# A state-space scan whose barred places are added by TensorE, with its rows loaded a stage earlier, and an expert combination with six slots

## The reference, cut to what matters

```python
def ssd_scan(x, dt, A, Bm, Cm):
    a_cs = jnp.cumsum(dt * A, axis=2)
    seg = a_cs[:, :, :, None, :] - a_cs[:, :, None, :, :]
    mask = jnp.tril(jnp.ones((CHUNK, CHUNK), dtype=bool))[:, :, None]
    Lmat = jnp.exp(jnp.where(mask, seg, -jnp.inf))
    xdt = x * dt[..., None]
    scores = jnp.einsum('bclhn,bcshn->bclsh', Cm, Bm) * Lmat
    y_diag = jnp.einsum('bclsh,bcshp->bclhp', scores, xdt)
    states = jnp.einsum('bclhn,bclh,bclhp->bchpn', Bm, decay_to_end, xdt)
    ...
    y_off = jnp.einsum('bclhn,bchpn,bclh->bclhp', Cm, prev, jnp.exp(a_cs))
# the end: two expert rows per token, weighted, gated, added to h, normalised
out = jnp.zeros((T, D)).at[row_tok].add(row_w[:, None] * yb)
h = h + gate2 * out
y = rmsnorm(h, final_g)
```

## Time and profile before

| | us | of the span |
|---|---|---|
| PE busy | 2977.3 | 82% |
| DVE (VectorE) busy | 2391.4 | 66% |
| ACT (ScalarE) busy | 1554.2 | 43% |
| POOL (GpSimd) busy | 558.5 | 15% |
| scan's stage, first instruction to the backward carry | 1601.2 to 1925.5 | 9% |
| combination, first load to the end | 3488.2 to 3628.8 | 4% |

### The profile page before, as it was taken

One profiled execution on the slowest core, in us unless ns is written; L12 is line 12 of the kernel. 1 busy time (PEld: TensorE's weight loads), 2 busy tenths in 40 slices (PEclk: granted clock), 3 DMA queues, 4 the chain that ended last, 5 costly groups with the idle time before them and its releaser, 6 DMA issues. The chain is left out here.

```text
span 3628.8 us, 41802 instructions
## 1 busy us (share of the span) xinstructions
PE 2977.3 (82%) x12653; PEld 1939.6 (53%) x12653; DVE 2391.4 (66%) x2967; ACT 1554.2 (43%) x1752; POOL 558.5 (15%) x413
## 2 busy tenths in 40 slices
PE   6999999489999999967783799819999999999920
PEld 3666666334444444434442455407777777777720
DVE  2555555347777777748996344347887888887855
ACT  2323332013333333343221122107788777777743
POOL 0000000000000000006660000042222222222224
PEclk8999999669999999988985899859999999999965
DMA  6112121521011110120005233345577776568347
GB/s 241 47 38 66 46 54 42 171 41 33 21 35 35 32 34 20 29 87 1 0 0 190 96 120 117 113 174 188 211 255 265 289 264 234 203 249 313 114 169 275
DMA packets 238793, 445.74 MB, mean 123 GB/s; under 512 B 22658, under 2 KB 96478, under 8 KB 237966
## 3 DMA queue, kind: packets, MB, share of 16 engines
q1 hardware_dynamic: 222141, 397.16, 32.6%
q0 software_dynamic: 16592, 47.84, 3.7%
HBM read 366.93 MB, written 86.40 MB: 125 GB/s over the span
## 5 line engine op out<-in xcount | busy, mean ns | idle before, releaser
L2090 DVE TENSOR_TENSOR weights_rest<-w,weights_rounded 128x2048 fp32r<-128x2048 f32 x314 | 716.3, 2289 | 191.8 <-ACT weights_rounded L2025 191.7
L2025 ACT ACTIVATE weights_rounded<-w 128x2048 fp32r x314 | 598.4, 1913 | 148.6 <-PE ps_up L1949 93.8
L823 ACT ACTIVATE probs<-ps_scores 128x1024 f32<-128x1024 f32 x260 | 266.1, 1023 | 503.8 <-PE ps_scores L754 442.0
L846 DVE TENSOR_REDUCE part_max<-ps_max 128x1 f32<-128x512 f32 (+1 forms) x528 | 338.0, 678 | 193.8 <-PE ps_max L731 193.7
L1949 PE MATMUL ps_up<-weights_rounded,block_T_rounded 128*128 128x512 f32 x832 | 339.6, 408 | 28.5 <-DVE weights_rest L2090 24.0
L430 PE MATMUL ps_proj<-w_in,n1T 128*128 128x512 f32 (+2 forms) x1152 | 348.0, 460 | 6.5 <-PEq L108 6.5
L1949 PE MATMUL ps_up<-weights_rounded,block_T_rest 128*128 128x512 f32 x832 | 327.4, 394 | 0.0
L1949 PE MATMUL ps_up<-weights_rest,block_T_rounded 128*128 128x512 f32 x832 | 326.1, 392 | 0.0
L764 PE MATMUL ps_attn<-probs,v 128*64 128x512 f32 x1040 | 283.7, 625 | 0.0
L430 PEld LDWEIGHTS ps_proj<-w_in,n1T 128*128 128x128 f32 x1152 | 197.8, 193 | 144.9 <-issue 130.0
L1498 PE MATMUL ps_out<-x_and_B,mix_T 128*128 128x512 f32 x576 | 255.7, 603 | 11.2 <-DVE mix_T L1539 11.2
(11 more groups left out here) (335 smaller groups left out, 4695.4 us busy)
## 6 DMA issues: line engine op xcount, KB each, us to landing
w<-in_w SPq DMA_DIRECT2D x96, 2048.0 KB, 10.7
expert_rows<-scratch_y SPq DMA_DIRECT2D x36, 512.0 KB, 5.0
w_ada_rest<-in_w_ada SPq DMA_DIRECT2D x5, 2048.0 KB, 16.0
scratch_qT<-qT_stage SPq DMA_DIRECT2D x18, 512.0 KB, 3.5
q_for_max<-scratch_qT SPq DMA_DIRECT2D x36, 256.0 KB, 5.7
q_rounded_twice<-scratch_qT SPq DMA_DIRECT2D x36, 256.0 KB, 4.3
mix_rows<-scratch_mix SPq DMA_DIRECT2D x18, 512.0 KB, 4.3
scratch_h<-h_rows SPq DMA_DIRECT2D x18, 512.0 KB, 2.6
```

What stands on the lines that cost most here:

```text
L823: act.activation(pf[:, slot(p, n), :], ps_s[:, n % 2, :], ACT.Exp).then_inc(exp_done, 1)
L846: nc.vector.tensor_reduce(mx[:, p, n // H, n % H:n % H + 1], ps_m[:, n % 2, 0:PART], AX.X, ALU.max).then_inc(m_taken, 1)
L2025: act.activation(split_piece(wh, s), raw_piece(s, buf[0]), ACT.Copy).then_inc(hi_done, 1)
L2090: nc.vector.tensor_tensor(split_piece(wl, s), raw_piece(s, buf), split_piece(wh, s).bitcast(F32), ALU.subtract).then_inc(lo_done, 1)
```

## The change

Three things. (1) The rows, masks and small constants of the scan are loaded in sample attention, behind its first three loads, into memory set aside before it; each channel group has a semaphore of its own, and SiLU stands before the exponentials of the sums. (2) `segment` and `mask` are gone. PE adds to the spread sums a matrix with 0 at allowed and -1e9 at barred places (rounded identity times `barred`, broadcast over four heads), and ScalarE takes the exponential per head with the row's negative sum as bias. `weights` multiplies by the unmasked C times B, which `rows` now takes from PSUM too. (3) The combination has six slots and is written out tile by tile; the tile's weights are read where they lie.

```diff
@@ attention_phase, SP
             load_for_max(1, 1)
+            if g:
+                load_scan(sp)
+        def load_scan(sp):
+            for name in ("dt_bias", "a_log", "d_skip"): ...
+            for c in range(XC):
+                for a, b, col in ((0, S_PROMPT, CONV_BASE[0]), (S_PROMPT, T, CONV_BASE[1])):
+                    sp.dma_start(dst, rows[:, c, col:col + b - a]).then_inc(S["ssm_in"][c], 16)
@@ ssm_phase, ScalarE
             own.link(act.activation(work[:, 3], work[:, 2], ACT.Ln))
+            for c in range(XC):
+                act.wait_ge(loaded[c], 32)
+                act.activation(v, v, ACT.Silu).then_inc(silu_done, 1)
             act.wait_ge(sums_ready, 3)
...
             def exps(c, p, d):
-                act.wait_ge(seg_ready, c * 2 + d + 1)
-                act.activation(e[:, p, d], e[:, p, d], ACT.Exp).then_inc(e_ready, 1)
+                act.wait_ge(sm_ready, c + 1)
+                act.wait_ge(bc_ready, c * 2 + d + 1)
+                wait(act, yd_ready, c - 1)
+                for h in range(H):
+                    last = act.activation(e[:, p, d, h, :], b_a[:, h * P:(h + 1) * P], ACT.Exp, bias=sm[:, p, NACS, d * H + h:d * H + h + 1])
+                last.then_inc(e_ready, 1)
@@ ssm_phase, PE: spread
-                wait(pe, seg_ready, c * 2 + d)
+                wait(pe, e_ready, c * 2 + d)
                 for n in range(2):
+                    nc.tensor.matmul(b_a[...], masks[:, 2, :], sacs[...], start=True, stop=False)
+                    last = nc.tensor.matmul(b_a[...], identr[:, :], bars, start=False, stop=True)
@@ ssm_phase, VectorE
+            nc.vector.tensor_copy(identr[:, :], S["ident"][:, :])
+            nc.vector.tensor_scalar(barred[:, :, :], masks[:, 0:2, :], -1.0, 1.0e9, ALU.add, ALU.mult)
+            nc.vector.tensor_scalar(stats[:, :, NACS, :], stats[:, :, ACS, :], -1.0, None, ALU.mult)
...
                 if more:
                     stage(c + 1, 1 - p)
-                    mask(c + 1, 1 - p)
-                    segment(c + 1, 1 - p, 0)
                 carry_on(c, p)
                 if more:
-                    segment(c + 1, 1 - p, 1)
                     weights(c + 1, 1 - p, 0)
                     weights(c + 1, 1 - p, 1)
                 add_up(c, p)
@@ combine_phase
+    RING = 6
             load(0)
             ...
+            for t in range(NT):
+                if t + RING - 1 < NT:
+                    load(t + RING - 1)
+                sp.wait_ge(o_ready, t + 1)
+                sp.dma_start(dst, o[:, t % RING, :]).then_inc(stored[t % RING], 16)
```

More of the change, by code:

```diff
@@ L914, in ssm_phase @@
     HG = SSM_H // SSM_G
-    ACS, EA, DT, DTDE, CD = range(5)
+    ACS, EA, DT, DTDE, CD, NACS = range(6)
     with ctx:
@@ L953, in ssm_phase @@
         block = ctx.enter_context(nc.Block())
[L954 to L967, removed]
         @block.gpsimd
@@ L1226, in _ @@
             stage(0, 0)
-            mask(0, 0)
-            for d in range(2):
-                segment(0, 0, d)
             for d in range(2):
@@ L2142, in _ @@
                 rest_weights(i, 13, after)
-def tiles_by_three(eng):
-    for t in range(3):
-        yield t, t, 0
-    with eng.Fori(1, NT // 3 - 1) as i:
-        for u in range(3):
-            yield i * 3 + u, u, i
-    for t in range(NT - 3, NT):
-        yield t, t % 3, t // 3
 def combine_phase(nc, I, S, R, O):
     ctx = ExitStack()
+    RING = 6
     with ctx:
@@ L2224, in _, with weigh @@
             own = Tally(act, act_own)
-            def weigh(t, p, turn):
-                act.wait_ge(y_in[p], turn * 32 + 32)
-                act.wait_ge(ws_ready, t + 1)
-                act.activation(y[:, p, 0, :], y[:, p, 0, :], ACT.Identity, scale=ws[:, p, 0:1]).then_inc(a_ready, 1)
-            weigh(0, 0, 0)
-            for t, p, turn in tiles_by_three(act):
-                own.at(t)
-                if at := ahead(t, p, turn, 1):
-                    weigh(*at)
+            def weigh(t):
+                act.wait_ge(y_in[t % RING], 32 * turn(t))
+                act.activation(y[:, t % RING, 0, :], y[:, t % RING, 0, :], ACT.Identity, scale=S["weights"][:, 0, t:t + 1]).then_inc(a_ready, 1)
@@ L2236, in _ @@
+            weigh(0)
+            for t in range(NT):
+                if t + 1 < NT:
+                    weigh(t + 1)
                 act.wait_ge(res_ready, t + 1)
-                own.link(act.activation(junk[:, :], o[:, p, :], ACT.Square, accum_out=st[:, p, 0:1]))
-                act.activation(st[:, p, 1:2], st[:, p, 0:1], ACT.Sqrt, scale=1.0 / D, bias=S["eps"][:, :]).then_inc(st_ready, 1)
+                own.link(act.activation(junk[:, :], o[:, t % RING, :], ACT.Square, accum_out=st[:, t % 3, 0:1]))
+                act.activation(st[:, t % 3, 1:2], st[:, t % 3, 0:1], ACT.Sqrt, scale=1.0 / D, bias=S["eps"][:, :]).then_inc(st_ready, 1)
@@ L2264, in _ @@
+            add_rows(0)
+            for t in range(NT):
+                if t + 1 < NT:
+                    add_rows(t + 1)
+                dve.wait_ge(gated, t + 1)
+                dve.wait_ge(h_in[t % RING], 16 * turn(t))
+                wait(dve, stored[t % RING], 16 * (t // RING))
+                nc.vector.tensor_tensor(o[:, t % RING, :], yg[:, t % 3, :], h[:, t % RING, :], ALU.add).then_inc(res_ready, 1)
+                if t == 0:
+                    dve.wait_ge(consts_in, 48)
                 dve.wait_ge(st_ready, t + 1)
-                nc.vector.reciprocal(st[:, p, 2:3], st[:, p, 1:2]).then_inc(inv_ready, 1)
+                nc.vector.reciprocal(st[:, t % 3, 2:3], st[:, t % 3, 1:2]).then_inc(inv_ready, 1)
```

164 lines of the change are left out of this document (72 added, 92 removed).

## The result

The changed kernel took 3575.79 us (median of 4 runs, 3574.65 to 3579.04) against 3635.12 (4 runs, 3630.17 to 3638.28) for the kernel before: a ratio of 0.9839, 95% interval 0.9822 to 0.9856. The forecast was 3579. The profiled execution after has a span of 3574.0 us, 54.8 less than before.

| us | before | after | forecast |
|---|---|---|---|
| preparation, barrier to GpSimd's first block of C | 35.2 | 20.7 | -14.4, came -14.5 |
| loop, from there to the end of the last y | 288.9 | 275.7 | -19, came -13.2 |
| combination | 140.6 | 119.3 | -18.5, came -21.3 |
| all other stages, whose work is unchanged | 3164.1 | 3158.3 | 0, came -5.8 |

A forecast was written before the change was run, and what follows sets the result against it. It took GpSimd's pass with its waits to set the scan's chunk and VectorE's round the new combination: 3630.65 - 14.4 - 19 - 18.5 = 3578.8, predicted 3579 us, with 8 in 10 runs from 3558 to 3598.

The forecast's parts named there:

- preparation: Scan's preparation: early loads and SiLU ahead of the exponentials start GpSimd's first chunk sooner, -14.4 us (-13 to -15).
- loop: Scan's loop: GpSimd's pass with its waits sets a chunk, 14.4 us against 15.5, so -19 us (0 to -32).
- combination: Combination: loads five tiles ahead leave VectorE's round, 5.70 us a tile against 6.79, so -18.5 us (0 to -20).
- rival D: Sample attention: its second tile's q waits behind the moved loads, giving back up to 20 us; 3593 us, chance 0.06.
- the 45 us of the first tile: Sample attention: tile 1 begins over 45 us after tile 0, covering the moved loads' 20 us, so cost 0.
- rival B: Loop: the port does not hold up the weights; PE's 13.5 us sets the chunk, -34 us, 3564 us; chance 0.14.
- -1.1, over 17 steps: Loop: each chunk falls from 15.5 to 14.4 us, -1.1, over 17 steps -19 us.
- 9.26 + 1.4: Loop, GpSimd's pass a chunk: 9.26 us of its own uncontended work plus 1.4 pushed in by VectorE's operations.
- rival E: Loop: PE becomes the bound at a granted clock below 0.78 and the kernel gets slower, up to 3793 us; chance 0.05.
- 13.5: Loop: PE's busy us a chunk at full granted clock with four added products, up from 12.54 (13.0 to 14.3).
- 349 GB/s: Combination: DMA rate worked out as 304/0.87, making a tile's transfers 6.0 us, 0.3 longer than VectorE's round.
- rival C: Combination: bound by the DMA engines, share 0.87 near full, so no gain there; 3597 us, chance 0.14.

The follow-up runs named there:

- experiment 6: Changed kernel with GpSimd's fifth scaled copy of x (the skip copy) made by ScalarE in eight small copies: 3567.57 us.
- experiment 9: Changed kernel with GpSimd's diagonals made in two operations, one for each direction, each with its own semaphore: 3545.69 us.
- experiment 12: Changed kernel with the diagonals in halves, the skip copy on ScalarE and the combination's gate on VectorE, together: 3517.15 us.
- experiment 2: Changed kernel with three slots in the combination in place of six, still written out tile by tile: 3598.12 us.
- experiment 4: Changed kernel with the second-row addition moved into VectorE's wait for the root, and the gate multiplication moved from GpSimd to VectorE: 3566.73 us.
- experiment 3: Changed kernel with VectorE's second-row addition of the next tile moved into its wait for ScalarE's root: 3585.25 us.

## Why the prediction was right

The three stages together came 49.0 us shorter, where the sum had 51.9; the combination's 2.8 made up half of the loop's shortfall of 5.8, and the unchanged stages added 5.8 that no step claimed. So the closeness of 3575.79 to 3579 is in part luck, and the terms are the better test.

**Preparation: right, -14.5 for -14.4.** The chain of single durations held (SiLU done at 1613.4, 17.2 us after the barrier, as worked out). Sample attention did not pay: 838.5 us with the 16 loads in its queue, 838.8 before, so rival D is out. That the 45 us of the first tile cover the loads fits this and was not tested.

**Loop: the mechanism right, the size not: -13.2 for -19.** GpSimd's pass with its waits was the thing to follow (experiments 6, 9 and 12), weights wait for GpSimd (2661 ns, so rival B is out), and ScalarE's pass is 2.17 for 2.2. The term that was mis-sized is "-1.1, over 17 steps". By the rows above, GpSimd's pass is 151.77/15 = 10.1 us busy, where the forecast had 9.26 + 1.4; 3.8 of waiting for the statistics, for 3.7; and 9.5/15 = 0.6 of waiting for PE, which the forecast put at nothing: 14.5 in all, for 14.4. The first 15 steps after the first y took 218.6 us in place of 232.6, so 14.0 less where the forecast had 16.5; two of them took 16.0 and 15.9 after PE's wait and lower clock, some 3 us together. The last two were never 15.5 long: 12.5 and 7.9 before, 11.4 and 9.2 after. The very last ran at a granted clock of 0.57; in two kernels with the same scan (experiments 2 and 4) it took 6.2 at 1.00, and their loops are 17 us shorter than before. So part of the shortfall is this profile's luck. The forecast priced the clock only as a disaster (rival E), not as a small toll inside the steps. E did not come: the granted clock was 0.94 over 216 us, with PE busy for 187.35 of them.

PE's "13.5" a chunk was too high, though the sum did not use it: the kernel with all three of experiment 12 keeps the bars and takes 11.7 us a step. So what rival B would have given is priced too low, and at full granted clock the margin of GpSimd's pass over PE was larger than the forecast thought.

That VectorE's two clamps, 4.4 us a chunk, would return about 1 us stands: part of the time went from waits of clamps into waits of weights, on the same port. The Trainium skill, SBUF — State Buffer, section "SBUF: two separate sides", calls the port pair that VectorE and GpSimd share an exclusive lock, held for the whole instruction; the row of 4.01 us above agrees, to 0.14 us.

**Combination: right, -21.3 for -18.5.** VectorE's round with its wait for the root was the bound, at 5.62 for 5.70 us (-1.4 over 17 steps); that the port stands close behind it (experiment 3) the forecast did not say. The first residual, 16.4 us after the stage's start instead of 17.9, gave 1.5. What was wrong is a side estimate: 349 GB/s, taken from a stretch in which the loads waited for slots, was no limit of the queues. They moved 414 to 417 GB/s, so rival C had no ground; experiment 4 shows that they were not the bound even at 5.07 us a tile, though a share of 1.03 shows no room beyond it.

## What to carry to other kernels

Where VectorE and GpSimd share work on SBUF, follow the pass of the pair, not VectorE's busy time: an operation taken off VectorE returns only what the pass loses. Here the change's own edit of the loop returned 13 us, diagonals in shorter pieces 33 and one copy moved to ScalarE 14 to 16; in the combination, work moved from GpSimd even to VectorE, the busier engine, returned another 13. In these kernels the longer waits of PE were followed by a lower granted clock, so an edit that made PE's neighbours faster lengthened the loop; with halved diagonals it no longer did. A bandwidth read off a stretch that waits for buffers is what was asked for, not what the queues can do.

## What was not expected of the hardware

- Cutting one 3.6 us operation of GpSimd into two, which take 1.89 us each undisturbed and 2.38 on the mean, took 33 us off the loop.
- Work taken away made the loop longer: with one exponential in place of eight, ScalarE has 30 passes of 1.02 us instead of 2.17, some 34 us less, and the loop took 5.5 us more (its first 15 steps 8.7), with a long and a short step in turn.
- The 16 DMA engines moved 414 to 417 GB/s with loads and stores mixed, at a share of 1.02 to 1.03.
